# The latent attention loop of a fused transformer kernel: turns and value products three tiles behind the scores instead of two

## The chip, the cores and the metric

The kernel runs on one core of one Trainium2 chip. The metric is the device time of one execution in microseconds (us); lower is better. PE stands for TensorE's matmuls, PEld for its weight loads, DVE for VectorE, ACT for ScalarE, POOL for GpSimd and SP for SyncE, whose queue issues most transfers.

## What is computed

The program is a block with dilated attention, spatial gating and a mixture of experts, followed by a block with two layers (a retention and state-space mixer, then latent attention, each with a gated feed-forward part). The change lies in the latent attention of the last layer: 16 heads, 512 queries and 768 keys (256 of the context and 512 of the sequence), with 64 + 32 query and key elements and 64 value elements a head.

```python
def mla_mixer(a_ctx, a_lat, ...):                      # MLA_HEADS = 16, QK_NOPE = 64, QK_ROPE = 32, V_HEAD = 64
    q_c, k_c, v_c = mla_project(a_ctx, w_in, q_norm_w, w_uq, kv_norm_w, w_ukv, None)
    q_l, k_l, v_l = mla_project(a_lat, w_in, q_norm_w, w_uq, kv_norm_w, w_ukv, rope)
    k_all = jnp.concatenate([k_c, k_l], axis=1)
    v_all = jnp.concatenate([v_c, v_l], axis=1)
    ...
    o_l = lax.map(lambda qb: softmax_attention(qb, k_all, v_all), q_blocks)
```

The products run in float32 split into a high and a low part, three matmuls for one product (`three`, L221).

## The kernel before, in words

Every engine has its own instruction stream, written out by hand in Python and run strictly in order. The streams meet through semaphores: `wait_ge(S(name), k)` holds the engine's whole queue until the k-th event of that name has happened. `heads_pe` (L3497), `heads_act` (L3576) and `heads_dve` (L3674) hold the latent heads for PE, ACT and DVE.

The 16 heads with 4 query tiles of 128 rows each are 64 units, n = 0 to 63; unit n is tile n % 4 of head n // 4 (`units`, L3356). Each of the three streams is a loop over n, and what one iteration of each holds fixes the order of the work:

- **PE, iteration n:** *scores n* (six matmuls at L142, 3 of 512 and 3 of 256 columns, two PSUM buffers; they wait for the exponential of n - 2). Then the *turns* of an older unit: six 128x128 transposes at L154, four into PSUM bank 4 and two into bank 5. They wait for that unit's scaled exponentials (`prob2`), and each half for the copy that empties its bank of the unit before (`pT_act`, `pT_dve`). Once in four iterations a *value product* of a whole head follows (24 matmuls at L3550, bank 6). Last come side jobs by tables of iteration numbers (L3391 to L3398).
- **ACT, iteration n:** the copy of four turned blocks (`turned`, L3615, L135), before the exponential, or behind it where the turned unit is the first tile of a head; there it also waits for the value product of the head before. Then exp of n (L132), then the two copies of a finished value product out of bank 6 (`o2_copy`, to tile MIXb, L3638), then ACT's part of the side jobs.
- **DVE, iteration n:** the row maximum of n (L123), the reciprocal (L126) and scaling (L116) of unit n - 1, the copy of the two other turned blocks (L129), then DVE's part of the side jobs.

The side jobs make queries, keys and values of later heads. *Key job* `k_nope_pe` at n in `KN_AT`, 12 matmuls, then two casts on ACT and two subtractions on DVE; *query job* `q_nope_pe`, two halves of nine matmuls at L3471 at n and n + 1 for n in `QN_AT`, then two casts and two subtractions; *rope turn* `q_pe_turn` at n in `PT_AT`, four transposes, then two casts and two subtractions; *value job* `v_pe` in `V_AT`; *rope query job* `q_pe_pe` in `QP_AT`. Jobs that write banks 6 and 7 wait for the consumers of earlier ones (`taken`, L3448), and the key, value and rope query jobs also for `o2_copy` of every value product issued so far:

```python
            if n in KN_AT:
                taken(p)
                p.wait_ge(S("o2_copy"), 2 * count(p, "o2"))
                k_nope_pe(p, KN_AT[n])
```

Exponentials go to three SBUF buffers in turn (`pb`, L3360: two in tile X, one in tile R). `OH_AT` and `WO_AT` hold casts of finished outputs and of output weights on ACT, with POOL subtracting behind them, for the projection that follows the loop (L2876).

Of the kernel before, what the change touches and what calls it, by code (L numbers as in the profile page):

```python
# [231 lines left out]
def program(nc, A, out):  # L232
    S = Sems(nc, FOLLOWS)
# [11 lines left out]
    con, ada = at("con", 6144, 1338), at("ada", 7584, 192)  # L245
# [7 lines left out]
    R, X = at("R", E0 + 12288, 12288), at("X", E0 + 24576, 6144)  # L253
# [587 lines left out]
    ml = lambda n: (sm[:, 2 * (n % 8):2 * (n % 8) + 1], sm[:, 2 * (n % 8) + 1:2 * (n % 8) + 2])  # L841
# [2266 lines left out]
    for l in range(2):  # L3108
        n = 0
# [246 lines left out]
    units = [(n // 4, n % 4) for n in range(64)]  # L3356
    vm = AT1[:, 0:3072].rearrange("p (t d) -> p t d", t=6)
    qpads = R[:, 11008:12160].rearrange("p (t d) -> p t d", t=4)
    qx, qpad = [qpads[:, t, :] for t in range(4)], qpads[:, :, 0:32]
    pb = [X[:, 4608:5376], X[:, 5376:6144], R[:, 10240:11008]]  # L3360
    pTm = AT1[:, 3072:6144].rearrange("p (b q) -> p b q", b=6)
    SC = 96.0 ** -0.5

# [30 lines left out]
    KN_AT = {4: 1, 11: 2, 16: 3, 28: 4, 31: 5, 40: 6, 48: 7}  # L3394
    PT_AT = {5: 1, 13: 2, 19: 3, 29: 4, 34: 5, 44: 6, 52: 7}
    WP_AT, WQ_AT = {20: 0, 21: 1, 22: 2}, {23: 0, 24: 1, 25: 2}
    OH_AT = {51: (0, 1), 53: (2, 3), 58: (4,), 59: (5,), 60: (6,), 66: (7,)}
    WO_AT = {54: 0, 55: 0, 56: 1, 57: 1, 61: 2, 62: 2, 63: 3, 64: 3}  # L3398
    QB = [[7, 1, 6, 0], [7, 6, 7, 6]]

# [96 lines left out]
    def heads_pe(p):  # L3497
# [12 lines left out]
        p.wait_ge(S("q_high"), 2)  # L3510
        p.wait_ge(S("q_low"), 2)
        v_pe(p, 0)
        for n in range(67):
            if n < 64:
                h, t = units[n]
                e = h % 2
# [9 lines left out]
                for t0, ln in ((0, 512), (512, 256)):  # L3526
                    p.acc(PS[:, 512 * b + t0:512 * b + t0 + ln],
                          three(qs, [(k2(g, e, 0)[ALL[e], t0:t0 + ln], k2(g, e, 1)[ALL[e], t0:t0 + ln])]),
                          inc=S("score2") if t0 else None)
            if 2 <= n < 66:  # L3530
                x = pb[(n - 2) % 3]
                p.wait_ge(S("prob2"), n - 1)
                p.wait_ge(S("k_pe_low"), 2)
                p.wait_ge(S("pT_act"), n - 2)
                p.turns([(bk(4, 128, 128 * b), x[:, 128 * b:128 * b + 128]) for b in range(4)], ident, S("p2_T"))
                p.wait_ge(S("pT_dve"), n - 2)
                p.turns([(bk(5, 128, 128 * b), x[:, 512 + 128 * b:640 + 128 * b]) for b in range(2)], ident, S("p2_T"))
            if n >= 3 and units[n - 3][1] == 3:
                h = units[n - 3][0]
                p.wait_ge(S("v_take"), 6 * (h // 8) + 6)  # L3540
                p.wait_ge(S("q_pe_copy"), count(p, "q_pe"))
                p.wait_ge(S("k_high"), 2 * count(p, "k_nope"))
                p.wait_ge(S("k_low"), 2 * count(p, "k_nope"))
                p.wait_ge(S("q_pe_low"), 2)
                p.wait_ge(S("pT_act"), n - 2)
                p.wait_ge(S("pT_dve"), n - 2)
                p.wait_ge(S("o2_copy"), 2 * h)
                for b in range(6):
                    for e in range(2):
                        ins = p.e.matmul(PS[64 * e:64 * e + 64, 512 * 6:512 * 6 + 256], vm[:, b, 64 * (h % 8):64 * (h % 8) + 64],  # L3550
                                         pTm[:, b, 256 * e:256 * e + 256], start=b == 0, stop=b == 5)
                p.up(ins, S("o2"))
# [23 lines left out]
    def heads_act(a):  # L3576
# [36 lines left out]
            q_pe_split(0, e)  # L3613
        v_take(0)
        def turned(n):  # L3615
            t = units[n - 2][1]
            a.wait_ge(S("p2_T"), 2 * (n - 2) + 1)
            a.wait_ge(S("o2"), units[n - 2][0])
            a.cast(pTm[:, 0:4, 128 * t:128 * t + 128], bk(4).rearrange("p (b q) -> p b q", b=4), inc=S("pT_act"))

        for n in range(67):
            if 2 <= n < 66 and units[n - 2][1]:
                turned(n)
            if n < 64:
                x, (m, l) = pb[n % 3], ml(n)
                b = 2 * (n % 2)
                a.wait_ge(S("top2"), n + 1)
                a.wait_ge(S("p2_T"), 2 * (n - 2))
                a.fn(x, PS[:, 512 * b:512 * b + 768], ACT.Exp, inc=S("exp2"), bias=m, accum_out=l)
            if 2 <= n < 66 and units[n - 2][1] == 0:  # L3630
                turned(n)
            if n >= 3 and units[n - 3][1] == 3:
                h = units[n - 3][0]
                r0 = 64 * (h % 2)
                a.wait_ge(S("o2"), h + 1)
                a.wait_ge(S("q_nope"), 8 if h >= 12 else 0)
                for e in range(2):
                    a.cast(oT[r0:r0 + 64, h // 2, 256 * e:256 * e + 256], PS[64 * e:64 * e + 64, 512 * 6:512 * 6 + 256], inc=S("o2_copy"))  # L3638
# [35 lines left out]
    def heads_dve(v):  # L3674
# [23 lines left out]
        for e in range(2):  # L3698
# [1 line left out]
            v.wait_ge(S("k_pe_high"), e + 1)  # L3700
            v.tt(k2(0, e, 1)[PE_[e], :], PS[PE_[e], 2048:2816], k2(0, e, 0)[PE_[e], :].bitcast(F32), ALU.subtract, inc=S("k_pe_low"))
            q_pe_split(0, e)
        for n in range(67):
            if n < 64:
                b = 2 * (n % 2)
                v.wait_ge(S("score2"), n + 1)
                v.wait_ge(S("exp2"), n - 7)
                v.red(ml(n)[0], PS[:, 512 * b:512 * b + 768], ALU.max, neg=True, inc=S("top2"))
            if 1 <= n <= 64:
                x, (m, l) = pb[(n - 1) % 3], ml(n - 1)  # L3710
                v.wait_ge(S("exp2"), n)
                v.recip(l, l)
                v.settle()
                v.ts(x, x, l, None, ALU.mult, inc=S("prob2"))
            if 2 <= n < 66:
                t = units[n - 2][1]
                v.wait_ge(S("p2_T"), 2 * (n - 2) + 2)
                v.wait_ge(S("o2"), units[n - 2][0])
                v.copy(pTm[:, 4:6, 128 * t:128 * t + 128], bk(5, 256).rearrange("p (b q) -> p b q", b=2), inc=S("pT_dve"))
            if n in QP_AT:  # L3720
                for t in QP_AT[n]:
# [200 lines left out]
```

## Time and profile before

| | value |
|---|---|
| median of 3 runs | 2356.7 us (2356.0 to 2361.01) |
| the profiled execution's own time | 2356.67 us |
| its span in the trace | 2354.8 us |
| PE busy | 2224.1 us, 94% of the span, 12894 matmuls |
| DVE busy | 1164.3 us, 49% |
| ACT busy | 774.4 us, 33% |
| POOL busy | 215.5 us, 9% |
| latent head loop | from 1654.9 us (scores 0) to 1925.6 us (last value product) |

The span begins with the first instruction and ends with the last; the execution's own time is 1.9 us longer. Matmuls overlap one another in the pipeline, so a row's duration is longer than the distance to the next row. In a timeline row the bracket at the end says how long the engine had been idle before it and what released it.

### The profile page before, as it was taken

What the parts mean: (1) busy time and instruction counts of PE and PEld (TensorE: products, weight loads), DVE (VectorE), ACT (ScalarE), POOL (GpSimd) and SP (SyncE); (2) the same over time, 40 slices, a digit from 0 to 9 for tenths busy, and PEclk for the clock granted to TensorE, in tenths of its full rate; (3) what the DMA queues carried; (4) which work ended last, traced back from release to release, by engine and by line L of the source; (5) the groups of instructions that cost most, each with busy time, mean ns of one, the idle gap of its engine ahead of it and who ended that gap; (6) DMA issues with size and microseconds to landing.
All of it is one profiled execution on the core that took longest, in us unless ns stands there. A gap on an engine that the chain in (4) does not pass through costs nothing.

```text
span 2354.8 us, 31075 instructions
## 1 busy us (share of the span) xinstructions
PE 2224.1 (94%) x12894; PEld 1720.2 (73%) x12894; DVE 1164.3 (49%) x1852; ACT 774.4 (33%) x1323; POOL 215.5 (9%) x195
## 2 busy tenths in 40 slices
PE   7999999888999998999999999999989889999997
PEld 5674864334779896788888888868777667788886
DVE  3234642222865787634424334345676655444444
ACT  2335311112443464331121111224656554222222
POOL 0000011110141270000000000002011050000000
PEclk9999999999999999999999999999999999999999
DMA  9947789999411213121212121211010103232321
GB/s 353 367 168 266 266 320 404 417 412 374 145 38 64 81 55 143 38 89 54 67 59 72 54 72 45 81 48 49 1 59 15 52 25 99 90 107 90 102 96 54
DMA packets 147227, 317.28 MB, mean 135 GB/s; under 512 B 16534, under 2 KB 77310, under 8 KB 134544
## 3 DMA queue, kind: packets, MB, share of 16 engines
q1 hardware_dynamic: 135808, 284.72, 33.7%
q0 software_dynamic: 10400, 27.38, 3.2%
q10 hardware_dynamic: 880, 3.20, 0.3%
q8 instruction: 102, 1.67, 0.3%
q14 instruction: 37, 0.30, 0.0%
HBM read 408.54 MB, written 15.79 MB: 180 GB/s over the span
## 4 chain that ended last, share of the span: by engine, by line
PE 76%; DVE 11%; DMA 6%; ACT 5%; issue 1%; SPq 1%; POOL 0%; DVEq 0%; ACTq 0%
PE PS L142 35%; PE PS L2948 11%; PE PS L721 4%; PE PS L154 3%; PE PS L1465 3%; PE PS L1758 3%; PE PS L2876 2%; PE PS L3550 2%; PE PS L1016 2%; PE PS L1477 2%; PE PS L148 2%; PE PS L531 2%; PE PS L3471 2%; DVE X L112 1%; DMA AT<-in_w_ada_dram 1%
## 5 line engine op out<-in xcount | busy, mean ns | idle before, releaser
L142 PE MATMUL PS<-at,wH 128*128 128x512 f32 (+1 forms) x2144 | 563.2, 352 | 1.8 <-DVE at L112 1.8
L142 PEld LDWEIGHTS PS<-at,wH 128*128 128x128 f32 x2144 | 378.2, 189 | 56.8 <-DVE at L112 1.3
L142 PE MATMUL PS<-at,rest 128*128 128x512 f32 (+1 forms) x1072 | 376.4, 351 | 0.0
L2948 PE MATMUL PS<-wH,ac 128*128 128x512 f32 x880 | 278.0, 393 | 3.5 <-DVE hn L112 3.5
L112 DVE TENSOR_TENSOR rest<-ring,wH 128x2048 fp32r<-128x2048 f32 x66 | 150.3, 2290 | 209.6 <-ACT wH L135 209.0
L142 PEld LDWEIGHTS PS<-at,rest 128*128 128x128 f32 x1072 | 202.7, 189 | 27.2
L2948 PEld LDWEIGHTS PS<-wH,ac 128*128 128x128 f32 x880 | 165.2, 188 | 43.5 <-DVE hn L112 8.7
L135 ACT CAST wH<-ring 128x2048 fp32r<-128x2048 f32 x66 | 124.6, 1906 | 199.8 <-PE PS L2948 199.8
L2948 PE MATMUL PS<-rest,ac 128*128 128x512 f32 x440 | 171.5, 390 | 0.0
L112 DVE TENSOR_TENSOR hn<-PS,gate 128x512 f32<-128x512 f32 x120 | 83.0, 691 | 104.8 <-PE PS L2948 99.4
L135 ACT CAST ac<-sil 128x1536 fp32r<-128x1536 f32 (+1 forms) x22 | 27.8, 1264 | 295.5 <-DVE sil L112 295.5
L112 DVE TENSOR_TENSOR sil<-sil,PS 128x512 f32<-128x512 f32 x66 | 39.5, 598 | 172.0 <-PE PS L142 172.0
L2948 PEld LDWEIGHTS PS<-rest,ac 128*128 128x128 f32 x440 | 82.7, 188 | 17.0 <-issue 0.7
L132 ACT ACTIVATE sil<-PS 128x512 f32<-128x512 f32 x66 | 34.6, 526 | 172.9 <-PE PS L142 172.9
L1465 PE MATMUL PS<-ring,AT 128*32 128x512 f32 x288 | 87.5, 613 | 3.6 <-DMA R<-in_w_gate_up_dram 3.2
L112 DVE TENSOR_TENSOR H<-H,hn 128x512 f32<-128x512 f32 x120 | 83.0, 692 | 4.1
L135 ACT COPY R<-PS 128x512 f32<-128x512 f32 (+4 forms) x105 | 47.4, 471 | 110.7 <-PE PS L142 56.2
L142 PE MATMUL PS<-Rr 96*128 96x512 f32 (+3 forms) x384 | 80.7, 345 | 1.3 <-ACT Rr L135 1.3
L154 PE MATMUL PS<-con,R 128*128 128x128 f32 (+1 forms) x452 | 66.5, 278 | 14.3 <-DVE R L116 8.1
L154 PEld LDWEIGHTS PS<-con,R 128*128 128x128 f32 (+1 forms) x452 | 50.6, 139 | 39.1 <-DVE R L116 12.0
L123 DVE TENSOR_REDUCE sm<-PS 128x1 f32<-128x768 f32 x64 | 60.9, 951 | 35.4 <-PE PS L142 34.9
L1465 PE MATMUL PS<-R,AT 128*32 128x512 f32 x400 | 71.9, 593 | 5.3 <-DMA HIw<-in_w_gate_up_dram 2.4
(480 smaller groups left out, 4376.1 us busy)
## 6 DMA issues: line engine op xcount, KB each, us to landing
R<-in_w_gate_up_dram SPq DMA_DIRECT2D x25, 1024.0 KB, 13.6
R<-in_w_gate_up_dram ACTq DMA_DIRECT2D x25, 1024.0 KB
ring<-in_w_ffn_gate_dram SPq DMA_DIRECT2D x22, 1024.0 KB, 5.4
ring<-in_w_ffn_up_dram SPq DMA_DIRECT2D x22, 1024.0 KB, 5.4
ring<-in_w_ffn_down_dram SPq DMA_DIRECT2D x22, 1024.0 KB, 4.9
ring<-in_w_gate_up_dram SPq DMA_DIRECT2D x18, 1024.0 KB, 10.6
ring<-in_w_gate_up_dram ACTq DMA_DIRECT2D x18, 1024.0 KB
ring<-in_w_ada_dram SPq DMA_DIRECT2D x16, 1024.0 KB, 7.5
```

Source lines behind the costliest of these rows:

```text
L112: return self.up(self.e.tensor_tensor(dst, a, b, op), inc)
L123: return self.up(self.e.tensor_reduce(dst, a, AX, op, negate=neg), inc)
L135: return self.up(self.e.copy(dst, src), inc)
L142: ins = self.e.matmul(out, l, r, start=k == 0, stop=k == len(pairs) - 1)
L148: ins = self.e.matmul(o, l, r, start=True, stop=True)
L154: ins = self.e.transpose(o, i_, ident[0:i_.shape[0], 0:i_.shape[0]])
L531: ins = p.e.matmul(PS[32 * j:32 * j + 32, 512 * b:512 * b + 512], cTv[:, k, 22 - 2 * q:54 - 2 * q], w[k // 4][:, k % 4, :], start=q == 0 a ...
L721: ins = p.e.matmul(bk(t), x, w[:, k, :], start=r == 0 and k == 0 and i == 0, stop=r == 1 and k == 3 and i == 2)
L1016: ins = p.e.matmul(bk(g % 3), x, w, start=k == 0 and i == 0, stop=k == 7 and i == 2)
L1465: ins = p.e.matmul(PS[32 * c:32 * c + 32, 512 * b:512 * b + 512], hgT[j % 2][:, 4 * third + k, 32 * c:32 * c + 32], expert_slot(g, third, ...
L1758: ins = p.e.matmul(bk(i % 4), x, y[:, k, :], start=b == 0 and k == 0 and n == 0, stop=b == 1 and k == 3 and n == 2)
L2948: ins = p.e.matmul(bk(4 + n_dn % 3), a_, b_, start=start and i == 0, stop=stop and i == len(terms) - 1)
```

## The change

The turns of unit n - 3 take the place of those of n - 2 in iteration n, on PE, and so do the two copies of turned blocks on ACT and DVE; the value product of a head follows in iteration n with n - 4 its last unit, not n - 3. All loops get one more iteration (68). A fourth buffer for exponentials lies in columns 256 to 1023 of the tile `con`, on constants that earlier stages used. The scaling on DVE stays one unit behind the maximum. The tables of side jobs keep their iteration numbers, but for the last entry of `OH_AT`.

```diff
@@ -3357,7 +3357,7 @@
     vm = AT1[:, 0:3072].rearrange("p (t d) -> p t d", t=6)
     qpads = R[:, 11008:12160].rearrange("p (t d) -> p t d", t=4)
     qx, qpad = [qpads[:, t, :] for t in range(4)], qpads[:, :, 0:32]
-    pb = [X[:, 4608:5376], X[:, 5376:6144], R[:, 10240:11008]]
+    pb = [X[:, 4608:5376], X[:, 5376:6144], R[:, 10240:11008], con[:, 256:1024]]
     pTm = AT1[:, 3072:6144].rearrange("p (b q) -> p b q", b=6)
     SC = 96.0 ** -0.5
 
@@ -3394,7 +3394,7 @@
     KN_AT = {4: 1, 11: 2, 16: 3, 28: 4, 31: 5, 40: 6, 48: 7}
     PT_AT = {5: 1, 13: 2, 19: 3, 29: 4, 34: 5, 44: 6, 52: 7}
     WP_AT, WQ_AT = {20: 0, 21: 1, 22: 2}, {23: 0, 24: 1, 25: 2}
-    OH_AT = {51: (0, 1), 53: (2, 3), 58: (4,), 59: (5,), 60: (6,), 66: (7,)}
+    OH_AT = {51: (0, 1), 53: (2, 3), 58: (4,), 59: (5,), 60: (6,), 67: (7,)}
     WO_AT = {54: 0, 55: 0, 56: 1, 57: 1, 61: 2, 62: 2, 63: 3, 64: 3}
     QB = [[7, 1, 6, 0], [7, 6, 7, 6]]
 
@@ -3510,7 +3510,7 @@
         p.wait_ge(S("q_high"), 2)
         p.wait_ge(S("q_low"), 2)
         v_pe(p, 0)
-        for n in range(67):
+        for n in range(68):
             if n < 64:
                 h, t = units[n]
                 e = h % 2
@@ -3527,23 +3527,23 @@
                     p.acc(PS[:, 512 * b + t0:512 * b + t0 + ln],
                           three(qs, [(k2(g, e, 0)[ALL[e], t0:t0 + ln], k2(g, e, 1)[ALL[e], t0:t0 + ln])]),
                           inc=S("score2") if t0 else None)
-            if 2 <= n < 66:
-                x = pb[(n - 2) % 3]
-                p.wait_ge(S("prob2"), n - 1)
+            if 3 <= n < 67:
+                x = pb[(n - 3) % 4]
+                p.wait_ge(S("prob2"), n - 2)
                 p.wait_ge(S("k_pe_low"), 2)
-                p.wait_ge(S("pT_act"), n - 2)
+                p.wait_ge(S("pT_act"), n - 3)
                 p.turns([(bk(4, 128, 128 * b), x[:, 128 * b:128 * b + 128]) for b in range(4)], ident, S("p2_T"))
-                p.wait_ge(S("pT_dve"), n - 2)
+                p.wait_ge(S("pT_dve"), n - 3)
                 p.turns([(bk(5, 128, 128 * b), x[:, 512 + 128 * b:640 + 128 * b]) for b in range(2)], ident, S("p2_T"))
-            if n >= 3 and units[n - 3][1] == 3:
-                h = units[n - 3][0]
+            if n >= 4 and units[n - 4][1] == 3:
+                h = units[n - 4][0]
                 p.wait_ge(S("v_take"), 6 * (h // 8) + 6)
                 p.wait_ge(S("q_pe_copy"), count(p, "q_pe"))
                 p.wait_ge(S("k_high"), 2 * count(p, "k_nope"))
                 p.wait_ge(S("k_low"), 2 * count(p, "k_nope"))
                 p.wait_ge(S("q_pe_low"), 2)
-                p.wait_ge(S("pT_act"), n - 2)
-                p.wait_ge(S("pT_dve"), n - 2)
+                p.wait_ge(S("pT_act"), n - 3)
+                p.wait_ge(S("pT_dve"), n - 3)
                 p.wait_ge(S("o2_copy"), 2 * h)
                 for b in range(6):
                     for e in range(2):
@@ -3613,24 +3613,24 @@
             q_pe_split(0, e)
         v_take(0)
         def turned(n):
-            t = units[n - 2][1]
-            a.wait_ge(S("p2_T"), 2 * (n - 2) + 1)
-            a.wait_ge(S("o2"), units[n - 2][0])
+            t = units[n - 3][1]
+            a.wait_ge(S("p2_T"), 2 * (n - 3) + 1)
+            a.wait_ge(S("o2"), units[n - 3][0])
             a.cast(pTm[:, 0:4, 128 * t:128 * t + 128], bk(4).rearrange("p (b q) -> p b q", b=4), inc=S("pT_act"))
 
-        for n in range(67):
-            if 2 <= n < 66 and units[n - 2][1]:
+        for n in range(68):
+            if 3 <= n < 67 and units[n - 3][1]:
                 turned(n)
             if n < 64:
-                x, (m, l) = pb[n % 3], ml(n)
+                x, (m, l) = pb[n % 4], ml(n)
                 b = 2 * (n % 2)
                 a.wait_ge(S("top2"), n + 1)
-                a.wait_ge(S("p2_T"), 2 * (n - 2))
+                a.wait_ge(S("p2_T"), 2 * (n - 3))
                 a.fn(x, PS[:, 512 * b:512 * b + 768], ACT.Exp, inc=S("exp2"), bias=m, accum_out=l)
-            if 2 <= n < 66 and units[n - 2][1] == 0:
+            if 3 <= n < 67 and units[n - 3][1] == 0:
                 turned(n)
-            if n >= 3 and units[n - 3][1] == 3:
-                h = units[n - 3][0]
+            if n >= 4 and units[n - 4][1] == 3:
+                h = units[n - 4][0]
                 r0 = 64 * (h % 2)
                 a.wait_ge(S("o2"), h + 1)
                 a.wait_ge(S("q_nope"), 8 if h >= 12 else 0)
@@ -3700,22 +3700,22 @@
             v.wait_ge(S("k_pe_high"), e + 1)
             v.tt(k2(0, e, 1)[PE_[e], :], PS[PE_[e], 2048:2816], k2(0, e, 0)[PE_[e], :].bitcast(F32), ALU.subtract, inc=S("k_pe_low"))
             q_pe_split(0, e)
-        for n in range(67):
+        for n in range(68):
             if n < 64:
                 b = 2 * (n % 2)
                 v.wait_ge(S("score2"), n + 1)
                 v.wait_ge(S("exp2"), n - 7)
                 v.red(ml(n)[0], PS[:, 512 * b:512 * b + 768], ALU.max, neg=True, inc=S("top2"))
             if 1 <= n <= 64:
-                x, (m, l) = pb[(n - 1) % 3], ml(n - 1)
+                x, (m, l) = pb[(n - 1) % 4], ml(n - 1)
                 v.wait_ge(S("exp2"), n)
                 v.recip(l, l)
                 v.settle()
                 v.ts(x, x, l, None, ALU.mult, inc=S("prob2"))
-            if 2 <= n < 66:
-                t = units[n - 2][1]
-                v.wait_ge(S("p2_T"), 2 * (n - 2) + 2)
-                v.wait_ge(S("o2"), units[n - 2][0])
+            if 3 <= n < 67:
+                t = units[n - 3][1]
+                v.wait_ge(S("p2_T"), 2 * (n - 3) + 2)
+                v.wait_ge(S("o2"), units[n - 3][0])
                 v.copy(pTm[:, 4:6, 128 * t:128 * t + 128], bk(5, 256).rearrange("p (b q) -> p b q", b=2), inc=S("pT_dve"))
             if n in QP_AT:
                 for t in QP_AT[n]:
```

Value products stood in iterations 6, 10, 14, ... 66 and stand in 7, 11, 15, ... 67 now. Two places on PE and one on ACT show it. L142 with tile Rr is scores, L154 with 128x128 x6 turns, L154 with 96x128 a rope turn, L3550 a value product.

PE, iterations 10 and 11 and the first matmul of the key job of iteration 11 (`L142 ... PS<-ATr,HI`), before:

```order
L142 MATMUL PS<-Rr 128x512 x3
L142 MATMUL PS<-Rr 128x256 x3
L154 MATMUL PS<-con,R 128x128 x6
L3550 MATMUL PS<-ATb 64x256 x12
L142 MATMUL PS<-Rr 128x512 x3
L142 MATMUL PS<-Rr 128x256 x3
L154 MATMUL PS<-con,X 128x128 x6
L142 MATMUL PS<-ATr,HI 128x256
```

and with the change:

```order
L142 MATMUL PS<-Rr 128x512 x3
L142 MATMUL PS<-Rr 128x256 x3
L154 MATMUL PS<-con 128x128 x6
L142 MATMUL PS<-Rr 128x512 x3
L142 MATMUL PS<-Rr 128x256 x3
L154 MATMUL PS<-con,X 128x128 x6
L3550 MATMUL PS<-ATb 64x256 x12
L142 MATMUL PS<-ATr,HI 128x256
```

The value product moved from between the two iterations to right ahead of the key job.

PE, from the rope turn of iteration 13 on, before:

```order
L154 MATMUL PS<-con,R 96x128 x4
L142 MATMUL PS<-Rr 128x512 x3
L142 MATMUL PS<-Rr 128x256 x3
L154 MATMUL PS<-con,X 128x128 x6
L3550 MATMUL PS<-ATb 64x256 x12
L142 MATMUL PS<-Rr 128x512 x3
L142 MATMUL PS<-Rr 128x256 x3
L154 MATMUL PS<-con,X 128x128 x6
```

and with the change:

```order
L154 MATMUL PS<-con,R 96x128 x4
L142 MATMUL PS<-Rr 128x512 x3
L142 MATMUL PS<-Rr 128x256 x3
L154 MATMUL PS<-con 128x128 x6
L142 MATMUL PS<-Rr 128x512 x3
L142 MATMUL PS<-Rr 128x256 x3
L154 MATMUL PS<-con,X 128x128 x6
L3550 MATMUL PS<-ATb 64x256 x12
```

The value product stands behind the second turns after the rope turn, no longer behind the first.

ACT, up to the casts of the key job of iteration 11 (`CAST Rr<-PS 64x768`; the ACTIVATE rows are exponentials, `COPY ATb` turned blocks, `COPY MIXb` the value product), before:

```order
L135 COPY ATb<-PS 128x4x128
L135 COPY MIXb<-PS 64x256 x2
L135 COPY ATb<-PS 128x4x128
L132 ACTIVATE R,sm<-PS,sm 128x768
L135 CAST Rr<-PS 64x768 x2
```

and with the change:

```order
L132 ACTIVATE R,sm<-PS,sm 128x768
L132 ACTIVATE con,sm<-PS,sm 128x768
L135 COPY ATb<-PS 128x4x128
L135 COPY MIXb<-PS 64x256 x2
L135 CAST Rr<-PS 64x768 x2
```

The copies of the value product moved from iteration 10 to iteration 11, directly ahead of the casts.

## Rows read from the trace of the kernel before

**Rows 1.** Busy time by stretch: length, PE, PEld, DVE, ACT, POOL, granted clock, DMA

```profile
1654.90:1925.60 270.70, 238.09 (x1528) 190.02 (x1528) 177.93 (x319) 165.24 (x321) 44.87 (x34) 0.99 0.09 33
```

**Rows 2.** Waits in the same stretch; us in total, times, longest

```profile
PE PS L154 <- DVE X L116: 8.7, 8, 1.9
...
PE PS L154 <- DVE R L116: 6.8, 6, 2.0
```

**Rows 3.** Timeline, iterations 12 and 13 on PE and DVE

```profile
1707.32 1.30 PE L142 MATMUL PS<-Rr 128*128 128x512 f32 x6
...
1708.71 0.96 DVE L123 TENSOR_REDUCE sm<-PS 128x1 f32<-128x768 f32 x1
...
1709.89 0.62 DVE L116 TENSOR_SCALAR R<-R,sm 128x768 f32<-128x768 f32 x1
1710.43 0.42 DVE L129 COPY ATb<-PS 128x256 f32<-128x256 f32 x1
...
1710.57 1.31 PE L154 MATMUL PS<-con,R 128*128 128x128 f32 x10 [1.96 <-DVE R L116]
```

**Rows 4.** Timeline, the value product of iteration 14 and the copies behind it

```profile
1713.38 1.40 DVE L112 TENSOR_TENSOR Rr<-PS,Rr 32x512 fp32r<-32x512 f32 x2 [0.61 <-ACT Rr L135]
...
1713.52 2.81 PE L3550 MATMUL PS<-ATb 128*64 128x256 f32 x24
1714.70 0.94 DVE L123 TENSOR_REDUCE sm<-PS 128x1 f32<-128x768 f32 x1
...
1716.26 1.32 PE L142 MATMUL PS<-Rr 128*128 128x512 f32 x6
...
1716.57 0.58 ACT L135 COPY ATb<-PS 128x512 f32<-128x512 f32 x1
1717.04 0.76 ACT L135 COPY MIXb<-PS 64x256 f32<-64x256 f32 x2
```

**Rows 5.** Timeline, iterations 43 to 46, behind a query job and behind a rope turn

```profile
1844.12 1.41 DVE L112 TENSOR_TENSOR Rr<-PS,Rr 64x512 fp32r<-64x512 f32 x2 [2.38 <-ACT Rr L135]
...
1847.42 0.87 PE L154 MATMUL PS<-con,X 128*128 128x128 f32 x6 [1.19 <-DVE X L116]
...
1848.13 0.60 PE L154 MATMUL PS<-con,R 128*96 128x128 f32 x4
...
1850.22 1.40 DVE L112 TENSOR_TENSOR Rr<-PS,Rr 32x512 fp32r<-32x512 f32 x2 [0.61 <-ACT Rr L135]
...
1851.55 0.94 DVE L123 TENSOR_REDUCE sm<-PS 128x1 f32<-128x768 f32 x1
...
1853.28 0.88 PE L154 MATMUL PS<-con,R 128*128 128x128 f32 x6 [1.78 <-DVE R L116]
```

**Rows 6.** Timeline, the rope turn of iteration 19

```profile
1736.55 0.61 PE L154 MATMUL PS<-con,R 128*96 128x128 f32 x4 [0.49 <-DVE Rr L112]
```

**Rows 7.** Timeline, a scaling beside POOL (iteration 22), and the rope query job of iteration 23

```profile
1743.34 1.29 DVE L116 TENSOR_SCALAR R<-R,sm 128x768 f32<-128x768 f32 x1
...
1744.69 0.88 PE L154 MATMUL PS<-con,R 128*128 128x128 f32 x6 [0.67 <-DVE R L116]
...
1751.66 0.36 PE L142 MATMUL PS<-gater,Hr 128*128 128x256 f32 x1 [1.44 <-POOL rest L112]
```

**Rows 8.** Timeline, the value job of iteration 35

```profile
1809.06 0.47 PE L142 MATMUL PS<-gater,ATr 128*128 128x512 f32 x1 [1.20 <-ACT Rr L135]
```

**Rows 9.** Busy time by stretch, the end of the loop (columns as in the first group)

```profile
1903.00:1918.00 15.00, 10.57 (x76) 7.83 (x74) 11.60 (x20) 12.17 (x26) 8.45 (x7) 1.00 0.00 1
1918.00:1925.50 7.50, 6.31 (x30) 4.00 (x30) 1.32 (x3) 1.84 (x4) 2.91 (x3) 0.55 0.00 0
```

**Rows 10.** Timeline, the last turns and the last two value products

```profile
1910.01 2.81 PE L3550 MATMUL PS<-ATb 128*64 128x256 f32 x24
...
1918.62 1.54 PE L154 MATMUL PS<-con,X 128*128 128x128 f32 x6 [1.82 <-DVE X L116]
...
1920.73 4.80 PE L3550 MATMUL PS<-ATb 128*64 128x256 f32 x24 [0.56 <-ACT ATb L135]
```

## The prediction, made before the changed kernel ran

> **What bounds the kernel now.** I read the busy time of the stretch first. The loop lasts 270.7 us and PE is busy 238.1 of them at a granted clock of 0.99, while DVE has 178 and ACT 165 [rows 1]. PE does the bulk, so its 32.6 us of pauses are all that an edit of this loop can win, and each pause has to be looked at by itself. The list of waits gives the share that the edit aims at: PE's turns waited for the scaling on DVE (L116, tiles X and R) 8.7 + 6.8 = 15.5 us, 14 times [rows 2]. If that sum went away, it would be 0.7% of the time. A measurement of this kernel can tell about 0.2% (4.7 us) from no change.
>
> Then the timeline of one such pause. Scores 13 are issued at 1707.32, and the turns of unit 11 begin at 1710.57 after 1.96 us of idling, when the scaling at 1709.89 has ended (1710.51). DVE had been late: maximum 12 began at 1708.71, behind the two subtractions of the key job of iteration 11. The row that decides this case is the one after the scaling: the copy that empties bank 5 of the unit before runs from 1710.43 to 1710.85 [rows 3], in the same iteration of the same queue. Turns need both.
>
> **Part 1: turns one unit older.** With the change, turns n - 3 in iteration n no longer wait for a fresh scaling. But they still wait for `pT_dve` at n - 3, the copy in DVE's iteration n - 1, and that copy still stands behind maximum n - 1 and scaling n - 2. DVE's order inside an iteration is the same, so what made DVE late makes the copy late. The first four transposes can go early, the last two cannot. Before: the turns start at 1710.57 [rows 3], and six that start after a wait keep PE for 0.71 us (1847.42 to 1848.13) [rows 5], so to 1711.28. After: two transposes start when the copy ends, at 1710.88 or so, and take a third of 0.71, 0.24, with a few hundredths to get going, so to 1711.16. That is 0.12 us a pause, and 14 pauses make **-1.7 us**. The bounds are 0, where DVE itself is the chain, and the whole 15.5 us, were the copy not there.
>
> The loop also starts with one group of turns less ahead of all that follows: **-0.6 us**, a little under the 0.71 of a group that had waited. The group comes back behind the last scores, where PE idles anyway: it waits 1.82 us before the last turns [rows 10].
>
> **Part 2: the value product moves against the side jobs.** This is the part that the words of the change don't name. A value product holds PE about 2.74 us (1713.52 to 1716.26) [rows 4]. It waits for nothing late, so in these microseconds DVE and ACT catch up. Before it stood in iterations with n % 4 = 2, now in those with n % 4 = 3, and the side jobs stayed.
>
> *What a side job costs without that cover.* Behind the rope turn of iteration 44 (1848.13) DVE subtracts until 1851.62, the next maximum starts at 1851.55, and the turns of iteration 46 wait 1.78 us. Behind the query job of iterations 41 and 42 the turns of 44 wait 1.19 us [rows 5]. *With cover:* behind the rope turn of iteration 13 the same subtractions run from 1713.38 and the maximum at 1714.70, all beside the value product, and scores 15 follow it at once [rows 4].
>
> So a job in iteration a is paid for in iteration a + 2, unless a value product stands in a + 1. Going through the tables:
> - Rope turns of 5, 13 and 29 had it (6, 14, 30) and lose it: 3 x 1.8 = **+5.4 us**, in the turns of 7, 15 and 31.
> - The query job of 8 and 9 had it (10) and loses it: **+1.2 us**, in the turns of 11.
> - The query jobs of 41/42 and 49/50 gain it (43, 51): 2 x 1.2 = **-2.4 us**.
> - The rope turn of 19 waited 0.49 us for a query job's subtractions [rows 6]; a value product now stands ahead of it: **-0.5 us**.
> - The turns of 22 waited 0.67 us, because POOL ran beside the scaling, which took 1.29 us and not 0.62 [rows 3, 7]. I keep that wait, since POOL's subtractions stay. The Trainium skill (SBUF — State Buffer, section Who interferes with whom) says that a DVE instruction in a two-port mode and a GpSimd instruction lock each other out of a shared port pair; the trace agrees by those two durations, and by that rule the fourth buffer, which is as much SBUF as the others, changes nothing.
>
> **Part 3: new waits for the copies out of bank 6.** The key jobs of iterations 11 and 31 and the jobs of 23 and 35 wait for both copies of every value product issued. Before, the last product lay one or more iterations back. Now it stands right ahead, in the same iteration. ACT first copies the turned blocks (1716.57), then the product (1717.04 to 1717.80), so the copies are done 1.54 us after the product's last issue at 1716.26 [rows 4].
> - Iterations 11 and 31: nothing was waited for, so 2 x 1.54 = **+3.1 us**. On ACT, the queue behind these copies holds only the casts of that same key job; DVE's subtractions and maximum 12 or 32 wait for them and shift along.
> - Iteration 23: the wait for POOL of 1.44 us [rows 7] is covered by the product and the new one takes its place: **+0.1 us**.
> - Iteration 35: the wait for ACT, 1.20 us [rows 8], goes, but three others come. The rope turn of 34 waits for the query job of 33, whose subtractions the product of 34 used to hide (0.5, as in [rows 6]); the turns of 35 are exposed (0.6, half of the 1.19, since the rope turn's own wait took the rest); and ACT reaches the copies only behind exponential 35, itself behind the subtractions of 34 (1.8 instead of 1.54). Together 2.9 - 1.2 = **+1.7 us**.
>
> **Part 4: the rest.** The copy, exponential and scaling of each unit are the same instructions. No DMA is added or moved, and SP's and POOL's queues are the same. Scores still need exponential n - 2, which the lag does not touch. The end of the loop: the last turns wait 1.82 us for the last scaling, and the last value product then ran at half clock, 4.80 us and not 2.81 [rows 9, 10]. Now the product of head 14 stands behind scores 63 and the copies behind it, but the chain of casts on ACT is as long. I take 0, between -2.0 (full clock) and +1.0.
>
> **The sum:** -1.7 - 0.6 + 5.4 + 1.2 - 2.4 - 0.5 + 0.1 + 3.1 + 1.7 = +6.3. For the stretches in which ACT's casts or POOL's subtractions set the pace (iterations 20 to 26 and 53 to 63), delays of PE are partly absorbed; from the pauses there of 0.67 to 1.44 us [rows 7, 8] I take off 0.5. That leaves **+5.8 us**. The profiled execution has 2356.67 us, the same as the median of the runs (2356.7): **2362.5 us**.
>
> **The rivals.**
>
> *The lag pays (faster).* If the copy of bank 5 is not what ends last, because the copies run early once the turns are older, each pause shrinks to what DVE's copy alone needs. Speaking for it: the waits for the scaling are the largest removable group [rows 2]. Against it: the copy ends 0.34 us *after* the scaling [rows 3]. Were all 15.5 us gone while parts 2 and 3 cost their 8.6 us (5.4 + 1.2 - 2.4 - 0.5 + 0.1 + 3.1 + 1.7), the time would be 2356.7 - 15.5 - 0.6 + 8.6 = 2349 us. It decides from the point at which more than 12.7 of the 15.5 us (8.6 - 0.6 + 4.7) are really removed. Chance 0.05.
>
> *The shifts even out (no change).* An uncovered side job costs its 1.8 us only if PE had been at the front. Should each of the four exposed places cost about half, as the backlog is carried into the next wait that exists anyway (the query job behind a key job), and the ACT copies be reached 0.5 us earlier, parts 2 and 3 fall by 3.3 + 1.5 us: 2362.5 - 4.8 = about 2358 us. The many jobs whose wait is relative to PE itself speak against it. Chance 0.30.
>
> *The clock falls (slower still).* The granted clock was 1.00 from 1903 to 1918, with PE busy 10.6 of 15 us, and 0.55 in the next 7.5 us [rows 9], that is at 1.2 GHz for most of it, after PE had idled, the last time for 1.82 us [rows 10]. There a value product cost 2.0 us more and a group of turns 0.7 (1.54 against 0.87) [rows 5, 10]. Around iterations 11 to 15 and 31 to 35 new pauses of 1 to 2 us stand close together. One such fall gives 2362.5 + 2.7 = 2365.2 us. The Trainium skill (TensorE: Matmul & The Clock Gate, section HAM oscillation — how this bites in real kernels) tells of a kernel whose idle gaps throttled PE again at every step; the trace agrees at the loop's end only, since pauses of 1.96 us did not do it elsewhere. Chance 0.10.
>
> **How the numbers follow.** The forecast's own case has 0.55. It covers 2359.5 to 2365: the three rope turns at 1.2 to 1.8 us, the two key jobs' waits at 1.0 to 1.6. About nine tenths of it lies above 2361.4, the bound of slower. Slower: 0.55 x 0.88 + 0.10 = 0.60 with a little from the even case. No change: 0.30 + 0.05 = 0.35. Faster: 0.05. The range runs from 2357.0 (the even case with the end of the loop at full clock) to 2367.0 (the clock case with part 1 at nothing), which leaves out the faster rival and the tails.
>
> **What would show it.** Right: the waits of turns for L116 are nearly gone and waits of turns for the copy at L129 (tile ATb) stand in their place, of about the same length; turns of 7, 11, 15 and 31 show pauses of 1 to 2 us; the first matmul of the key jobs of 11 and 31 waits some 1.5 us for ACT's MIXb copy; the turns of 44 and 52 show none. PE's busy time is unchanged and the loop is about 6 us longer. Wrong: if the turns' waits are gone with nothing in their place, part 1 is wrong; if the loop is as long as before although the value products wait as said, what evens out is in part 2.

## The result, and the profile after

| | before | with the change |
|---|---|---|
| median of 8 runs each | 2357.19 us (2354.54 to 2361.01) | 2367.78 us (2363.91 to 2369.41) |
| the profiled execution's own time | 2356.67 us | 2364.8 us |
| its span | 2354.8 us | 2362.9 us |
| scores 0 to the first matmul of the projection (L2876) | 271.4 us | 279.7 us |

The ratio is 1.0039 with a 95% interval of 1.003 to 1.0048, so +9.2 us (7.1 to 11.3): slower, and more than the 5.8 us forecast. (Differences worked out from the ratio are up to 1.7 us smaller or larger than those of the medians; below, both are given where it matters.) By the ratio the 2356.7 us that the forecast started from become 2365.9, inside the stated range of 2357 to 2367; the median of these eight runs itself lies 0.8 us above its upper end. The loop of the profiled execution accounts for 8.3 us.

First the busy time of the loop with the change, from scores 0 to the projection (columns as in [rows 1]):

```profile
1654.60:1934.30 279.70, 240.12 (x1528) 189.46 (x1529) 178.46 (x319) 166.31 (x323) 45.38 (x34) 0.99 0.09 32
```

PE has the same 1528 matmuls. Its pauses grew from about 33 to 39.6 us, and its busy time by 2 us; iterations 54 to 59, in which the clock fell (below), have 2.2 us more of it, the rest about the same as before. Now PE's waits in the same loop (total, times, longest):

```profile
PE PS L154 <- DVE ATb L129: 15.1, 13, 1.9
PE PS L142 <- ACT MIXb L135: 6.7, 4, 2.1
...
PE PS L154 <- ACT ATb L135: 3.9, 7, 1.5
```

This answers to [rows 2]. The 15.5 us in which the turns waited for the scaling (L116) have vanished, and 15.1 us in which they wait for the copy (L129) have appeared. Four waits for the copies of a value product, 6.7 us, are new.

The two sums are alike, but not all their waits stand at the same places. Nine places have one before and after, at the turns of 13, 21, 22, 26, 46, 53, 54, 58 (59 with the change) and 62: 10.2 us for the scaling became 9.3 us for the copy, 0.1 us less a pause. The other five of before, 5.3 us at the turns of 44, 52, 60 and 61 and at the last turns, no longer wait for DVE. Four at the turns of 7, 11, 15 and 31, 5.8 us, are new and belong to the moved value products. So only the nine show what the lag does to a pause; that the sums come out within 0.4 us of each other is chance.

The timeline of iterations 9 to 13 shows both kinds of wait, for the copy of turned blocks and for those of a value product. It is the stretch of [rows 3], with the value product now in iteration 11:

```profile
1700.45 0.96 DVE L123 TENSOR_REDUCE sm<-PS 128x1 f32<-128x768 f32 x1
1700.94 0.60 PE L154 MATMUL PS<-con,X 128*128 128x128 f32 x4
...
1701.64 0.62 DVE L116 TENSOR_SCALAR X<-X,sm 128x768 f32<-128x768 f32 x1
1702.18 0.42 DVE L129 COPY ATb<-PS 128x256 f32<-128x256 f32 x1
...
1702.65 0.44 PE L154 MATMUL PS<-con,X 128*128 128x128 f32 x2 [1.10 <-DVE ATb L129]
1703.02 2.81 PE L3550 MATMUL PS<-ATb 128*64 128x256 f32 x24
...
1705.93 0.59 ACT L135 COPY ATb<-PS 128x512 f32<-128x512 f32 x1 [1.44 <-PE PS L3550]
...
1706.54 0.76 ACT L135 COPY MIXb<-PS 64x256 f32<-64x256 f32 x2
...
1714.34 0.42 DVE L129 COPY ATb<-PS 128x256 f32<-128x256 f32 x1
...
1714.82 0.87 PE L154 MATMUL PS<-con,R 128*128 128x128 f32 x6 [1.86 <-DVE ATb L129]
```

Turns are now split into a group of four (x4), which starts with no scaling to wait for, and one of two (x2; where a rope turn follows at once, the row counts its four too, x6), which starts 0.05 us after the copy has ended at 1702.60. The turns of 11 pause for 1.10 us where before none did. The value product ends, ACT copies turned blocks and then the product until 1707.30, and only then can the key job of iteration 11 start:

```profile
1707.44 0.36 PE L142 MATMUL PS<-ATr,HI 128*128 128x256 f32 x1 [1.61 <-ACT MIXb L135]
```

Behind it the turns of 13 wait 1.86 us for the copy, where they had waited 1.96 for the scaling. The turns of 7 and the value job of 35 look like this:

```profile
1687.39 0.44 PE L154 MATMUL PS<-con,X 128*128 128x128 f32 x2 [1.55 <-DVE ATb L129]
...
1819.00 0.47 PE L142 MATMUL PS<-gater,ATr 128*128 128x512 f32 x1 [2.05 <-ACT MIXb L135]
```

And the turns of 44 (1855.94, behind the value product of 43) wait for nothing, where they had waited 1.19 us [rows 5]:

```profile
1852.04 2.81 PE L3550 MATMUL PS<-ATb 128*64 128x256 f32 x24
...
1855.94 0.82 PE L154 MATMUL PS<-con,X 128*128 128x128 f32 x6
```

### The profile page after: what moved, and what is told of

Same layout as the page of the kernel before. It is cut to its first block, busy times and chain, and to the rows that moved or that the text cites. A ratio compares the mean times of both kernels' runs of the same rounds, so it can differ in the third digit from the quotient of the medians.

```text
span 2362.9 us, 31076 instructions
## 1 busy us (share of the span) xinstructions
PE 2224.3 (94%) x12894; PEld 1721.0 (73%) x12894; DVE 1165.4 (49%) x1852; ACT 774.8 (33%) x1323; POOL 216.3 (9%) x195
## 4 chain that ended last, share of the span: by engine, by line
PE 75%; DVE 11%; DMA 7%; ACT 5%; issue 1%; SPq 1%; POOL 0%; DVEq 0%; ACTq 0%
PE PS L142 35%; PE PS L2948 11%; PE PS L721 4%; PE PS L154 3%; PE PS L1465 3%; PE PS L1758 3%; PE PS L2876 2%; PE PS L1016 2%; PE PS L148 2%; PE PS L3550 2%; PE PS L531 2%; PE PS L1477 2%; PE PS L3471 1%; DVE X L112 1%; DVE Rr L112 1%
## 5 line engine op out<-in xcount | busy, mean ns | idle before, releaser
L142 PE MATMUL PS<-at,wH 128*128 128x512 f32 (+1 forms) x2144 | 564.6, 352 | 0.7 <-DVE at L112 0.7
L142 PEld LDWEIGHTS PS<-at,wH 128*128 128x128 f32 x2144 | 379.4, 190 | 55.8 <-issue 1.1
L142 PE MATMUL PS<-at,rest 128*128 128x512 f32 (+1 forms) x1072 | 376.9, 352 | 0.0
L142 PEld LDWEIGHTS PS<-at,rest 128*128 128x128 f32 x1072 | 203.4, 190 | 27.0
L142 PE MATMUL PS<-Rr 96*128 96x512 f32 (+3 forms) x384 | 81.1, 347 | 1.3 <-ACT Rr L135 1.3
L142 PEld LDWEIGHTS PS<-Rr 96*128 96x128 f32 (+1 forms) x384 | 65.0, 189 | 15.6 <-issue 2.3
L154 PE MATMUL PS<-con,R 128*128 128x128 f32 (+1 forms) x422 | 63.1, 278 | 13.7 <-DVE ATb L129 3.7
```

The lines of the kernel that those rows point to most:

```text
L142: ins = self.e.matmul(out, l, r, start=k == 0, stop=k == len(pairs) - 1)
L154: ins = self.e.transpose(o, i_, ident[0:i_.shape[0], 0:i_.shape[0]])
```

## Where the microseconds went, along the loop

The start of scores n against the start of scores 0, from the two timelines, beside what the terms of the prediction add up to by then:

| up to scores | before | with the change | difference | forecast |
|---|---|---|---|---|
| 16 | 63.0 | 69.2 | +6.1 | +5.6 |
| 24 | 101.0 | 105.7 | +4.7 | +4.9 |
| 32 | 137.0 | 145.7 | +8.7 | +8.1 |
| 36 | 157.0 | 167.3 | +10.3 | +9.8 |
| 48 | 203.6 | 212.6 | +9.0 | +8.3 |
| 54 | 227.1 | 234.6 | +7.5 | +7.0 |
| 60 | 247.1 | 257.0 | +9.9 | +6.6 |
| projection | 271.4 | 279.7 | +8.3 | +5.8 |

Up to scores 54 the sum holds within 0.7 us. The error grows from 0.5 to 3.3 us between scores 54 and 60 and is 2.5 us at the projection, and the rows there show something that the sum did not contain:

```profile
1892.90 0.44 PE L154 MATMUL PS<-con 128*128 128x128 f32 x2 [1.55 <-DVE ATb L129]
1893.10 1.63 PE L142 MATMUL PS<-Rr 128*128 128x512 f32 x6
...
1894.62 1.71 PE L154 MATMUL PS<-con,X 128*128 128x128 f32 x6
...
1896.26 3.28 PE L3550 MATMUL PS<-ATb 128*64 128x256 f32 x24
```

Scores take 1.63 us and not 1.30, turns 1.71 and not 0.87, the product 3.28 and not 2.81. The busy times of two stretches (columns as before) name the cause:

```profile
1890.00:1900.00 10.00, 8.27 (x48) 5.45 (x47) 7.38 (x14) 6.45 (x14) 2.84 (x2) 0.83 0.30 111
1900.00:1922.00 22.00, 19.88 (x133) 14.88 (x134) 18.92 (x32) 19.66 (x41) 16.25 (x12) 1.00 0.00 1
```

The granted clock was 0.83 over ten microseconds, so the lower level of 1.2 GHz stood for about a third of them. PE had paused 1.55 us right before. That cost some 0.33 + 0.84 + 0.47 = 1.6 us. The end of the loop gave part of it back. The last value product took 3.50 us, against 4.80 before [rows 10], because less of it fell into the slow stretch at the end (clock at its lower level from 1928 to 1932, before from 1918 to 1925):

```profile
1929.95 3.50 PE L3550 MATMUL PS<-ATb 128*64 128x256 f32 x24 [0.57 <-ACT ATb L135]
```

## The experiments

My theory has three parts. The lag itself changes next to nothing, since the copy ends right after the scaling. Most of the loss comes from value products that moved against side jobs. The rest is the new waits for the copies out of bank 6. The rivals: the lag costs by itself, or the fourth buffer does. A further one, the clock, no edit here sets; its short falls are read from the trace of each run.

### The fourth buffer alone

```diff
-    pb = [X[:, 4608:5376], X[:, 5376:6144], R[:, 10240:11008]]
+    pb = [X[:, 4608:5376], X[:, 5376:6144], R[:, 10240:11008], con[:, 256:1024]]
```

with units modulo 4 in the three streams of the kernel before.

> The kernel before with only the fourth buffer added (pb in four parts, units taken modulo 4, turns and value products two units behind as before). Both my theory and the trace of the changed kernel say that the place of the buffer costs nothing: the same as before within 0.1%, 2357 us. Rival (tile con as target of ACT and DVE and source of PE's transposes, beside the identity that lies in the same tile, is slower): +2 us or more.

Measured: 2357.35 us (11 runs) beside 2357.35 for the kernel before, ratio 0.9998 (0.9989 to 1.0007). The buffer changes the time by no more than 0.1% either way. That rival is out.

### The changed kernel with the side jobs moved along

```diff
-    KN_AT = {4: 1, 11: 2, 16: 3, 28: 4, 31: 5, 40: 6, 48: 7}
+    KN_AT = {5: 1, 12: 2, 17: 3, 29: 4, 32: 5, 41: 6, 49: 7}
```

and all the other tables and the single steps in the same way, but for the value jobs of 0 to 2 and the last entry of `OH_AT`.

> The change as it is, but every table of side jobs (and the WO_AT and OH_AT casts, and the n == 3, 26 and 27 steps) one iteration later, so that side jobs and value products stand to each other as before the change, with turns still three units behind and the fourth buffer kept. My theory (the lag itself gives 0.12 us a pause, the slowdown is the value product moved against the side jobs): the 8.6 us of parts 2 and 3 go, the small gains of part 1 stay, about 2.3 us under the kernel before, 2355 us, with waits of the turns for the DVE copy (L129) of about 13 to 15 us in total still there. Rival (the lag or the buffer in tile con is itself what costs): no better than the changed kernel, about 2366 us.

Measured: 2354.82 us, ratio 0.9985 (0.9976 to 0.9994), so 3.5 us *faster* than the kernel before with the lag of three in it. In its trace the loop up to the projection takes 268.7 us, 2.7 less than before; the forecast for part 1 alone was -2.3. Both traces have the clock at its lower level for about 7 us at the end and nowhere else in the loop. PE's waits there:

```profile
PE PS L154 <- DVE ATb L129: 11.9, 11, 1.8
```

Here, with the jobs back beside their value products, the waits compare like with like: 15.5 us for the scaling became 11.9 us for the copy. That is less than the 13 to 15 us expected; 1.8 us went at the last turns, which had waited for the scaling and now wait for ACT's copies. No wait of PE for MIXb is left inside the loop. The lag is a small gain, and the whole loss, and more, came from what it stood next to.

### The kernel before with the side jobs moved the other way

The mirror: no lag, no fourth buffer, only the tables one iteration earlier (`KN_AT = {4: 1, 10: 2, 15: 3, 27: 4, 31: 5, 39: 6, 47: 7}` and so on).

> The kernel before (turns two units behind, three buffers, value products at n % 4 = 2), but the side jobs from iteration 7 on one iteration earlier, so that they stand to the value products as in the changed kernel; not shifted are the jobs of iterations 2 to 5, the jobs of 31, 32 and 34, and the casts from 51 on. My theory: slower than before without any lag or fourth buffer. Exposed turns behind the rope turns of 12 and 28 (2 x 1.8), behind the query job of 7/8 (1.2), the key job of 10 waits for ACT's copies (1.5), the value job of 34 too (0.9 more than now), against 2 x 1.2 + 0.5 us won behind the query jobs of 40/41, 48/49 and at the rope turn of 18: +4.4 us, about 2361.5. Rival (the lag or the buffer costs): the same as before, 2357.

Measured: 2365.11 us, ratio 1.0032 (1.002 to 1.0044). The loss appears without any of the change's own edits. It is larger than expected, +7.5 us against +4.4. The waits:

```profile
PE PS L154 <- DVE X L116: 14.6, 10, 1.9
PE PS L142 <- ACT MIXb L135: 4.9, 3, 1.7
PE PS L154 <- DVE R L116: 3.1, 4, 1.2
```

Turns wait 17.7 us for the scaling instead of 15.5, and there are three waits for MIXb, at the jobs of 10, 22 and 34. I had counted for 34 only the difference to the old wait. With the value job a step earlier than its rope turn, two more waits stand around it:

```profile
1818.33 0.64 PE L154 MATMUL PS<-con,R 128*96 128x128 f32 x4 [0.68 <-ACT ATb L135]
...
1821.16 0.47 PE L142 MATMUL PS<-gater,ATr 128*128 128x512 f32 x1 [0.49 <-DVE Rr L112]
```

Those 1.2 us belong to this kernel alone. The trace has two falls of the clock inside the loop as well, from 1791 to 1795 and from 1890 to 1894 (0.57 on the mean of each), behind pauses of 1.88 and 1.83 us. The first fell on a value product:

```profile
1790.09 0.88 PE L154 MATMUL PS<-con,X 128*128 128x128 f32 x6 [1.88 <-DVE X L116]
1790.89 4.50 PE L3550 MATMUL PS<-ATb 128*64 128x256 f32 x24
```

It took 4.50 us and not 2.81, 1.7 us more, and the second fall cost about as much. Against that, the end of the loop ran about 1.1 us shorter than before, with fewer matmuls at the lower clock. 4.4 + 1.2 + 3.3 - 1.1 is 7.8 us, beside 7.2 in the profiled loop and 7.5 by the ratio.

### Three rope turns one iteration later

```diff
-    PT_AT = {5: 1, 13: 2, 19: 3, 29: 4, 34: 5, 44: 6, 52: 7}
+    PT_AT = {6: 1, 14: 2, 19: 3, 30: 4, 34: 5, 44: 6, 52: 7}
```

> The changed kernel with three entries of PT_AT one iteration later: rope turns at 6, 14 and 30 instead of 5, 13 and 29, so that a value product stands in the iteration behind each. My theory: the pauses of the turns of 7, 15 and 31 (1.55 us each in the trace of the changed kernel) go, about 4.6 us less than the changed kernel, 2363 us against 2367.5; at 6 and 30 the wait for the key job's subtractions (1.8 and 1.2 us) moves from the rope turn to the turns behind it and stays. Rival (the pauses come from the lag, not from the place of the value product): no difference to the changed kernel.

Measured: 2363.42 us, ratio 1.0024 (1.0015 to 1.0034). By the medians that is 4.4 us under the changed kernel, by the two ratios 3.5 us; 4.6 were expected. In the trace scores 16 start 3.5 us earlier than in the changed kernel (65.7 against 69.2 after scores 0), which is the first two pauses. The wait for key subtractions moved from the rope turn to the turns of 6, as said (and at 30, where it lasts 1.84 us and not 1.2):

```profile
1683.52 0.44 PE L154 MATMUL PS<-con 128*128 128x128 f32 x2 [2.00 <-DVE ATb L129]
```

By scores 32 it is 4.4 us ahead. Then its profiled execution loses 1.6 us again, because PE ran at 0.83 of the clock from 1812 to 1822, behind a wait of 2.04 us, and another 1.4 us from scores 54 on, where its last value product ran slow for longer than the changed kernel's. So one profile shows 1.4 us of gain where ten runs show 4.4: the clock makes single profiles of this loop uncertain by some microseconds.

### The jobs that wait for the product's copies one iteration later

```diff
-    KN_AT = {4: 1, 11: 2, 16: 3, 28: 4, 31: 5, 40: 6, 48: 7}
+    KN_AT = {4: 1, 12: 2, 16: 3, 28: 4, 32: 5, 40: 6, 48: 7}
```

with the query job 32 to 33, rope turn 34 to 35 and the value jobs 35 to 37 to 36 to 38.

> The changed kernel with only those side jobs moved that waited for the value product's copies: key job 11 to 12, key job 31 to 32 with its query job 32 to 33, rope turn 34 to 35 and value jobs 35 to 37 to 36 to 38. My theory: the waits for MIXb at 11 (1.61), 31 (1.49) and 35 (2.05) and for the query job at 34 (0.49) go, ACT's wait at the value job (1.20) comes back: -4.4 us, 2363 us. The exposed turns of 7, 11, 15 and 31 stay. Rival (these waits only stand where others would end at the same time): within 1 us of the changed kernel.

Measured: 2360.76 us, ratio 1.001 (1.0002 to 1.0019), 7.0 us under the changed kernel (6.8 by the ratios) against 4.4 expected. In the traces scores 59 start 4.4 us earlier than in the changed kernel (246.9 against 251.3), which is the sum. Each of the two traces has one fall of the clock by then, here from 1720 to 1724 and there from 1894 to 1897, so they cancel. The other 1.3 us of the profile lie between there and the projection (5.7 in all), where this execution had no slow stretch: its last value product took 2.81 us and not 3.50, and the turns ahead of it 0.85 and not 1.47. That the medians differ by 7.0 us no single trace explains.

```profile
1925.26 2.81 PE L3550 MATMUL PS<-ATb 128*64 128x256 f32 x24 [0.56 <-ACT ATb L135]
```

### The copy ahead of the scaling, with the lag of three

```diff
...
                 v.red(ml(n)[0], PS[:, 512 * b:512 * b + 768], ALU.max, neg=True, inc=S("top2"))
+            if 3 <= n < 67 and units[n - 3][1]:
+                t = units[n - 3][1]
+                v.wait_ge(S("p2_T"), 2 * (n - 3) + 2)
+                v.wait_ge(S("o2"), units[n - 3][0])
+                v.copy(pTm[:, 4:6, 128 * t:128 * t + 128], bk(5, 256).rearrange("p (b q) -> p b q", b=2), inc=S("pT_dve"))
             if 1 <= n <= 64:
...
-            if 3 <= n < 67:
+            if 3 <= n < 67 and units[n - 3][1] == 0:
```

> The changed kernel with DVE's copy of the turned blocks ahead of the reciprocal and scaling in every iteration whose turned unit is not a head's first tile. My theory (with the lag of three, the turns wait for that copy and for nothing else of DVE's): the copy ends 0.80 us earlier in its iteration. Pauses followed by a value product (turns of 7, 11, 15, 31) shrink by 0.8 each; behind the nine others the next scores then wait for the exponential, which is done about 2.05 us after the maximum starts, against 2.4 now, so 0.35 each. -3.2 - 3.1 = -6.3 us, 2361 against 2367.5 us. Rival (the copy is only the last of several equal waits, and the scaling, now later, or the exponential takes over at once): within 1 us of the changed kernel.

Measured: 2360.69 us, ratio 1.0009 (1.0 to 1.0019), 7.1 us under the changed kernel, 6.3 expected. The waits of the turns for the copy fell to less than half, and the next ones in line (ACT's copy, the exponential) took little. Besides the two below, the last but one turns wait 1.46 us for the scaling, where they had waited as long for ACT's copy:

```profile
PE PS L154 <- DVE ATb L129: 6.2, 8, 1.0
PE PS L154 <- ACT ATb L135: 4.5, 11, 0.8
...
PE PS L142 <- ACT X L132: 0.8, 3, 0.3
```

The edit changes only the copy's place in DVE's queue. So in the changed kernel more than half of the turns' waits for the copy (8.9 of 15.1 us) came from the scaling that stands ahead of it.

### The same copy ahead of the scaling, with the lag of two

> The kernel before (turns two units behind) with only DVE's copy moved ahead of the scaling, as in e3. My theory: there the turns wait for the scaling, and the copy ahead of it makes it 0.4 us later; 14 pauses, so up to +4 us, about 2360 us. It shows that the copy can only go ahead because of the lag. Rival (the copy ahead is what helps, lag or not): 3 to 6 us faster than before.

Measured: 2365.89 us, ratio 1.0028 (1.0018 to 1.0037): slower than before by 8.3 us in the medians and 6.6 by the ratio, more than my +4. At the turns of 13 the wait grew from 1.96 to 2.29 us as expected, by the copy that now runs first:

```profile
1712.73 0.41 DVE L129 COPY ATb<-PS 128x256 f32<-128x256 f32 x1
...
1713.38 0.62 DVE L116 TENSOR_SCALAR R<-R,sm 128x768 f32<-128x768 f32 x1
...
1714.05 1.31 PE L154 MATMUL PS<-con,R 128*128 128x128 f32 x10 [2.29 <-DVE R L116]
```

But the number of such waits grew too, which I had not counted:

```profile
PE PS L154 <- DVE X L116: 13.3, 14, 2.1
PE PS L154 <- DVE R L116: 10.5, 8, 2.3
```

That is 23.8 us against 15.5. Seven groups of turns that had not waited (6, 8, 16, 20, 30, 40 and 48) now wait 0.41 to 0.47 us each, about the length of the copy: there the scaling used to end just in time. This trace too has two falls of the clock inside the loop (from 1746 and from 1893, behind 1.88 and 2.15 us), so not all of the loss is the waits. The copy ahead of the scaling gains 7.1 us with the older turns and loses without them.

### All together

The lag of three, every side job one iteration later, the copy ahead of the scaling.

> The lag of three with all side jobs one iteration later (as e1) and the copy ahead of the scaling (as e3). My theory: from the 2354.8 us of e1, eleven waits of the turns for the copy (11.9 us) shrink by 0.35 each, -3.9 us: 2351 us, faster than both kernels. Rival (the next wait takes all of it): 2355 us as e1.

Measured: 2349.9 us (8 runs) beside 2357.64, ratio 0.9961 (0.9948 to 0.9974): 9.2 us faster than the kernel before by the ratio, and faster than both kernels of this case; 2351 us were expected. The loop up to the projection takes 262.2 us against 271.4, some 1.3 us of which come from a shorter stretch at the lower clock at its end (1909 to 1913). The turns behind the key job, the place of [rows 3]:

```profile
1706.16 0.96 DVE L123 TENSOR_REDUCE sm<-PS 128x1 f32<-128x768 f32 x1
1707.04 0.41 DVE L129 COPY ATb<-PS 128x256 f32<-128x256 f32 x1
...
1707.51 0.44 PE L154 MATMUL PS<-con 128*128 128x128 f32 x2 [0.99 <-DVE ATb L129]
1707.68 0.62 DVE L116 TENSOR_SCALAR X<-X,sm 128x768 f32<-128x768 f32 x1
```

PE resumes at 1707.51, before the scaling has even begun. The pause is 0.99 us where it was 1.96 and 1.86. What the turns wait for now is spread over two engines:

```profile
PE PS L154 <- ACT ATb L135: 6.0, 11, 1.5
PE PS L154 <- DVE ATb L129: 4.0, 6, 1.0
```

## Why the prediction was right, point by point

- **Direction and mechanism:** right. At the nine places that wait before and after, 10.2 us for the scaling became 9.3 us for the copy. The mirrored experiment shows the slowdown without the lag, the shifted one shows the lag without the slowdown. The size is missed by more than half of the forecast (+9.2 against +5.8 us). That the two sums of waits (15.5 and 15.1) are of about the same length, as the prediction's list of signs has it, came in by luck, as said above.
- **Part 1 (-1.7 - 0.6):** right. Forecast -2.3, and -2.7 in the loop of the kernel in which only part 1 is left. Its timed ratio gives -3.5 us (-1.4 to -5.7).
- **Exposed rope turns (3 x 1.8):** the places were right, and the turns of 7, 15 and 31 each waited 1.55 us in their second group plus 0.02 to 0.14 in the first. Moving the three jobs gave back 3.5 us by the ratios and 4.4 by the medians.
- **Exposed query job (1.2):** 1.10 us at the turns of 11. **Covered ones (-2.4):** the wait at 44 is gone, and that at 52 too.
- **The waits for copies out of bank 6:** 1.61, 1.60, 1.49 and 2.05 us, forecast 1.54 (three times) and 1.8. Of the two small terms at iteration 35, the rope turn of 34 waits 0.49 us (forecast 0.5) and the turns of 35 show no wait (forecast 0.6).
- **The term that failed is Part 4** together with the rival of the clock. I priced the half-clock stretch as another outcome with a chance of 0.10, at 2.7 us. It came in the forecast's own case: one such stretch in iterations 54 and 55, about 1.6 us. The 2.5 us between the forecast's 5.8 and the profile's 8.3 us are these 1.6, 0.5 us of small errors up to scores 54, and 1.2 us more in iterations 54 to 60, where the forecast shrinks by 0.4 us and the loop grew by another 0.8, which I did not take apart; less 0.8 us at the end, where the last value product alone ran 1.3 us shorter than before and Part 4 had put nothing. PE's busy time, forecast as unchanged, is 2 us longer for it.
- **The lower end of the range** was worked out wrongly: the even case (2357.7 us) less the 2.0 us of full clock at the end is 2355.7, not 2357.0. Nothing hangs on it here.
- The median of the changed kernel lies 3 us above its profiled execution, that of the kernel before 0.5 us. The changed kernel's eight runs have mean clocks down to 0.988, against 0.991 in the profile. One of them has 0.992 and still took 2367.53 us. Over 31 runs of the kernel before, taken with the later experiments, the twelve with a mean clock of 0.988 or 0.989 took 2360.9 us on average and the nineteen with 0.990 or more 2356.9. So further stretches at the lower clock can make a difference of this size; no trace of such a run of the changed kernel shows them, and it stays open.

## What to carry to other kernels

When a wait is to be removed, look up what the waiting instruction needs next and when that is ready. Here the next release came 0.34 us later on the same engine, so an older unit bought 0.1 us a pause; moving the *next* instruction too (a 0.42 us copy ahead of a 0.62 us scaling) brought the larger part, 9.2 us with shifted tables where the lag alone had brought 3.5. And where side work is placed by iteration numbers against a long matmul group that hides it, a lag that moves this group by one iteration must move the tables too: the same kernel is 9.2 us slower than before with the old tables, and 3.5 us faster with shifted ones.

## What the runs showed of the hardware that I had not expected

The granted clock fell to 1.2 GHz for short stretches inside the loop in six of the ten profiles, behind pauses of PE of 1.55 to 2.25 us. There is one in the changed kernel (at 1893.9 behind 1.55 us), one with the waiting jobs moved (1720 behind 1.55 us) and one with the copy first (1818 behind 2.25 us). There are two in the mirrored kernel, two with the moved rope turns (1815 behind 2.04 us, 1890 behind 1.55 us) and two with the copy first and the lag of two. The kernel before, the one with four buffers, the one with shifted tables and the one with all together, which are also the four fastest, have none ahead of the loop's last iterations. Pauses of 1.86 to 1.96 us elsewhere were followed by full clock, so the length of a pause alone does not decide, and with one trace of each kernel it is not shown that the moved jobs make such falls more frequent. Where a fall lay on a value product it made it 1.7 us longer (4.50 against 2.81).

The Trainium skill (TensorE: Matmul & The Clock Gate, section A second HAM failure mode: psum-queue depth-cycling) describes frequent short idling between groups of matmuls that lets the throttle come and go. The traces agree so far as the clock falls and returns in a loop with pauses of this kind, at 0.83 over the ten microseconds from 1890 in the changed kernel; what in the pauses brings it about no run here tests. In such a loop a pause costs its own length and sometimes 1.6 us more, and only repeated runs average that.
